# Attention in head pairs on the halves of TensorE, with a fused score-and-maximum operation and an early opening of the output projection

## What is computed

```
scores = (q @ k.T) * HEAD_DIM ** -0.5 + bias        # per head; 256 queries, causal
p = exp(scores - max(scores)); p = p / sum(p)
o = p @ v
x = x + concat(o) @ w_o
```

## Time and profile before

| what | value |
|---|---|
| median of 3 runs | 1553.88 us (1550.59 to 1556.39) |
| the profiled execution: time | 1550.96 us |
| the profiled execution: span of the core | 1549.2 us |
| TensorE busy | 1468.2 us, 95% of the span |
| VectorE busy | 780.3 us, 50% |
| ScalarE busy | 573.7 us, 37% |
| mean granted TensorE clock | 0.983 |

### The profile page before, as it was taken

One profiled execution on the slowest core, in us unless ns is written; L12 is line 12 of the kernel. 1 busy time (PEld: TensorE's weight loads), 2 busy tenths in 40 slices (PEclk: granted clock), 3 DMA queues, 4 the chain that ended last, 5 costly groups with the idle time before them and its releaser, 6 DMA issues.

```text
span 1549.2 us, 28384 instructions
## 1 busy us (share of the span) xinstructions
PE 1468.2 (95%) x11254; PEld 1225.1 (79%) x11254; DVE 780.3 (50%) x1409; ACT 573.7 (37%) x929; POOL 294.6 (19%) x121
## 2 busy tenths in 40 slices
PE   7978999999999999999999999999999999989996
PEld 5857999999958999998999898998666666555553
DVE  4954888637674898733453645653322222212122
ACT  2244555445344655436655116444211111111110
POOL 0021222212201121233865001673000000000000
PEclk9989999999999999998999999999999999999998
DMA  8674455574534455652544212477999999999995
GB/s 312 234 275 157 163 164 173 191 255 139 164 137 136 147 174 184 203 175 82 177 137 137 69 55 74 166 256 268 427 424 426 423 425 426 426 427 424 423 426 222
DMA packets 72097, 375.82 MB, mean 243 GB/s; under 512 B 8128, under 2 KB 8384, under 8 KB 49984
## 3 DMA queue, kind: packets, MB, share of 16 engines
q1 hardware_dynamic: 72000, 374.43, 64.1%
HBM read 373.35 MB, written 1.05 MB: 242 GB/s over the span
## 4 chain that ended last, share of the span: by engine, by line
PE 61%; issue 13%; DVE 8%; DMA 8%; SPq 7%; ACT 2%; POOL 1%; POOLq 0%; DVEq 0%; ACTq 0%
PE lin L692 9%; PE lin L693 8%; PE lin L694 8%; DMA moe_low<-in_experts 7%; PE stat L1394 4%; PE mixp L1367 4%; PE mixp L1371 4%; SPq L609 4%; DVE mixers L2034 3%; PE lin L711 2%; PE stat L1327 1%; PE lin L1337 1%; PE stat L692 1%; PE mixp L692 1%; PE stat L693 1%
## 5 line engine op out<-in xcount | busy, mean ns | idle before, releaser
L692 PE MATMUL lin<-r_hi,w_hi 128*128 128x256 f32 x1464 | 426.4, 291 | 11.8 <-POOL w_lo L1838 5.1
L693 PE MATMUL lin<-r_lo,w_hi 128*128 128x256 f32 x1464 | 416.6, 285 | 0.0
L694 PE MATMUL lin<-r_hi,w_lo 128*128 128x256 f32 x1464 | 416.5, 284 | 0.0
L692 PEld LDWEIGHTS lin<-r_hi,w_hi 128*128 128x128 f32 x1464 | 283.4, 194 | 19.8 <-POOL w_lo L1838 6.7
L693 PEld LDWEIGHTS lin<-r_lo,w_hi 128*128 128x128 f32 x1464 | 283.4, 194 | 0.8
L694 PEld LDWEIGHTS lin<-r_hi,w_lo 128*128 128x128 f32 x1464 | 283.2, 193 | 0.0
L1842 POOL TENSOR_TENSOR w_lo<-ring,w_hi 128x1024 fp32r<-128x1024 f32 x71 | 175.4, 2482 | 199.3 <-ACT w_hi L1435 199.2
L1838 POOL TENSOR_TENSOR w_lo<-ring,w_hi 128x1024 fp32r<-128x1024 f32 x42 | 108.3, 2578 | 480.2 <-ACT w_hi L1441 297.9
L1871 DVE TENSOR_TENSOR w_lo<-ring,w_hi 128x1024 fp32r<-128x1024 f32 x126 | 156.5, 1247 | 84.9 <-ACT w_hi L1441 65.1
L1441 ACT ACTIVATE w_hi<-ring 128x1024 fp32r<-128x1024 f32 x124 | 129.6, 1049 | 57.3 <-PE mixp L694 49.0
L1435 ACT ACTIVATE w_hi<-ring 128x1024 fp32r<-128x1024 f32 x119 | 124.1, 1050 | 34.1 <-PE lin L694 16.7
(11 more groups left out here) (485 smaller groups left out, 2795.1 us busy)
## 6 DMA issues: line engine op xcount, KB each, us to landing
ring<-in_panels SPq DMA_DIRECT2D x272, 512.0 KB, 3.8
moe_low<-in_experts SPq DMA_DIRECT2D x64, 1024.0 KB, 22.6
moe_high<-in_experts SPq DMA_DIRECT2D x22, 2048.0 KB, 24.9
aring<-in_ada SPq DMA_DIRECT2D x24, 1024.0 KB, 6.3
ring<-in_experts SPq DMA_DIRECT2D x20, 1024.0 KB, 26.6
moe_high<-in_experts SPq DMA_DIRECT2D x20, 1024.0 KB, 21.9
cst<-in_experts SPq DMA_DIRECT2D x10, 1280.0 KB, 23.5
sq<-in_experts SPq DMA_DIRECT2D x10, 1024.0 KB, 29.5
```

The lines of the kernel that those rows point to most:

```text
L692: pe.matmul(o, w_hi[:, slot, c], r[0], start=start, stop=False, skip_group_check=True)
L693: pe.matmul(o, w_hi[:, slot, c], r[1], start=False, stop=False, skip_group_check=True)
L694: return pe.matmul(o, w_lo[:, slot, c], r[0], start=False, stop=stop, skip_group_check=True)
```

## The change

The attention loop goes over eight pairs of heads. Scores of both heads of a pair are issued alternately, on the two row halves and in two banks; the outputs of both heads alternately on the two column halves of one bank. In PE's order the scores of the next pair come first, then the outputs of the pair two back, the modulation group, and the transposes of the pair before. On VectorE one fused operation per block, `tensor_tensor_reduce`, adds the bias (now eight times as large), scales by minus one eighth, writes the negated scores and their minimum; ScalarE's exponential takes them with scale -1. The two heads' probabilities are scaled by one operation per block, with a broadcast reciprocal. Two `w_lo` splits of the output projection's panels are placed in turns 1 and 2. The first two panels of the projection are done tile by tile: six tiles before the last pair is transposed, one before its outputs, one after. The even layer's projection now opens with two panels as well.

```diff
-        "bias00": pattern_bias(0, 0), "bias10": pattern_bias(P, 0), "bias11": pattern_bias(P, P),
+        "bias00": HD ** 0.5 * pattern_bias(0, 0), "bias10": HD ** 0.5 * pattern_bias(P, 0), "bias11": HD ** 0.5 * pattern_bias(P, P),
...
+            def open_project(tiles, rows, first, last):
+
+                if first:
+                    for j in range(2):
+                        bank(split_panel(j))
+                for i in tiles:
+                    for j in range(2):
+                        b = (panels.n + j) % RING
+                        mm = split_matmul(lin[b][:, 0:T], (b, slice(i * P, (i + 1) * P)), [t[:, i, :] for t in rows],
+                                          first and i == tiles[0], last and i == tiles[-1])
+                        if last and i == tiles[-1]:
+                            mm.then_inc(panel_done, 1)
+                if last:
+                    panels.advance(2)
...
             pe.wait_ge(r_split, 1 + KH)
+            open_project(range(KD), (r_hi, r_lo), True, True)
             project((r_hi, r_lo))
...
+            def score_pair(j):
+
+                if j:
+                    pe.wait_ge(scores_read, j)
+                for part in range(2):
+                    for n in range(2):
+                        q, k = (qk1[64 * n:64 * n + 64, t, :] for t in (j, 8 + j))
+                        if part == 0:
+                            pe.matmul(mixbank(n)[:, 0:P], q[:, 0:P], k[:, 0:P], start=True, stop=True, skip_group_check=True)
+                        else:
+                            mm = pe.matmul(mixbank(n)[:, P:3 * P], q[:, P:T], k, start=True, stop=True, skip_group_check=True)
+                mm.then_inc(scores_ready, 1)
+
+            def outputs(g):
+
+                pe.wait_ge(pt_copied, 2 * g + 2)
+                if g >= 2:
+                    pe.wait_ge(o_copied, g - 1)
+                for c in range(3):
+                    for n in range(2):
+                        head = 2 * g + n
+                        o = lin[g % 2][64 * n:64 * n + 64, (0 if c == 0 else P):(P if c == 0 else T)]
+                        mm = pe.matmul(o, vt1[:, c // 2, head * HD:(head + 1) * HD],
+                                       pt1[:, 2 * (g % 2) + n, c * P:(c + 1) * P], start=c < 2, stop=c != 1, skip_group_check=True)
+                mm.then_inc(o_ready, 1)
+
+            def turn_probs(g):
+
+                pe.wait_ge(probs_ready, g + 1)
+                for n in range(2):
+                    if g:
+                        pe.wait_ge(pt_copied, 2 * g - 1 + n)
...
+            score_pair(0)
+            for j in range(PAIRS):
+                if j + 1 < PAIRS:
+                    score_pair(j + 1)
+                if j >= 2:
+                    outputs(j - 2)
+                modulation(lin[2], 16 + j, 1)
+                if j >= 1:
+                    turn_probs(j - 1)
+            outputs(PAIRS - 2)
+            pe.wait_ge(o_copied, PAIRS - 2)
             pe.wait_ge(modrow_ready, 3)
+            open_project(range(0, PAIRS - 2), (r_hi, r_lo), True, False)
+            turn_probs(PAIRS - 1)
+            pe.wait_ge(o_copied, PAIRS - 1)
+            open_project([PAIRS - 2], (r_hi, r_lo), False, False)
+            outputs(PAIRS - 1)
+            pe.wait_ge(o_copied, PAIRS)
+            open_project([PAIRS - 1], (r_hi, r_lo), False, True)
             project((r_hi, r_lo))
...
-                    if i == HEADS:
-                        split_hi(OUT1 + 1)
-            split_hi(OUT1 + 4)
-            modulation_row(lin[2][:, :], 2)
+            for j in range(HEADS // 2 + 1):
+                if j < HEADS // 2:
+                    act.wait_ge(scores_read, j + 1)
+                    if j >= 2:
+                        act.wait_ge(pt_ready, 2 * j - 2)
...
+                if j:
+                    g = j - 1
+                    for n in range(2):
+                        act.wait_ge(pt_ready, 2 * g + n + 1)
+                        if g >= 2:
+                            act.wait_ge(o_ready, g - 1)
+                        act.activation(pt1[:, 2 * (g % 2) + n, :], statbank(n)[:, 0:SC], ACT.Copy).then_inc(pt_copied, 1)
+                if j == HEADS // 2 - 1:
+                    modulation_row(lin[2][:, :], 2)
...
+            for j in range(HEADS // 2 + 2):
+                if j < HEADS // 2:
...
+                    for n in range(2):
+                        for c, (a0, a1) in enumerate(((0, P), (P, 3 * P))):
+                            m = 2 * (2 * j + n) + c
+                            ins = dve.tensor_tensor_reduce(s1[:, 2 * (j % 2) + n, a0:a1], mixbank(n)[:, a0:a1], bias[:, a0:a1],
+                                                           -HD ** -0.5, 3e38, ALU.add, ALU.min, mx1[:, m:m + 1])
+                    ins.then_inc(scores_read, 1)
+                if j in (1, 2):
+                    split_lo(OUT1 + 1 + j)
+                if 1 <= j <= HEADS // 2:
...
+                    link(dve.reciprocal(r1[:, 4 * g:4 * g + 4], l1[:, 4 * g:4 * g + 4]))
                     for c, (a0, a1) in enumerate(((0, P), (P, 3 * P))):
+                        ins = dve.tensor_tensor(p1[:, pair, a0:a1], p1[:, pair, a0:a1],
+                                                per_row(r1, g, c).unsqueeze(2).broadcast_to([P, 2, a1 - a0]), ALU.mult)
                     ins.then_inc(probs_ready, 1)
+                if j >= 2:
+                    g = j - 2
+                    dve.wait_ge(o_ready, g + 1)
+                    split_rows(g, lin[g % 2][:, 0:T]).then_inc(o_copied, 1)
             split_lo(OUT1 + 4)
```

More of the change, by code:

```diff
@@ L777, in route @@
                     mm.then_inc(ev("logits_ready"), 1)
+            def open_project(tiles, rows, first, last):
[11 more added lines that the diff above has]
+                    panels.advance(2)
             def project(rows, first=False):
                 if first:
-                    opening = [split_panel(j) for j in range(2)]
-                    for b in opening:
-                        bank(b)
                     for i in range(KD):
                         pe.wait_ge(h_ready, seen(h_ready))
-                        for b in opening:
-                            mm = split_matmul(lin[b][:, 0:T], (b, slice(i * P, (i + 1) * P)), [t[:, i, :] for t in rows],
-                                              i == 0, i == KD - 1)
-                            if i == KD - 1:
-                                mm.then_inc(panel_done, 1)
-                    panels.advance(2)
-                for m in range(2 if first else 0, KD):
+                        open_project([i], rows, i == 0, i == KD - 1)
+                for m in range(2, KD):
                     b = split_panel()
@@ L989, in _ @@
             pe.wait_ge(qk_ready, 16)
-            for i in range(HEADS + 3):
-                if i < HEADS:
-                    if i >= 2:
-                        pe.wait_ge(scores_read, i - 1)
-                    o = 64 * (i % 2)
-                    q, k = qk1[o:o + 64, i // 2, :], qk1[o:o + 64, 8 + i // 2, :]
-                    pe.matmul(mixbank(i)[:, 0:P], q[:, 0:P], k[:, 0:P], start=True, stop=True, skip_group_check=True)
-                    pe.matmul(mixbank(i)[:, P:3 * P], q[:, P:T], k, start=True, stop=True, skip_group_check=True)\
-                        .then_inc(scores_ready, 1)
-                if i < HEADS and i % 2 == 1:
-                    modulation(lin[2], 16 + i // 2, 1)
-                if 2 <= i <= HEADS + 1:
-                    g = i - 2
-                    pe.wait_ge(probs_ready, g + 1)
-                    if g >= 2:
-                        pe.wait_ge(pt_copied, g - 1)
+            def score_pair(j):
[9 more added lines that the diff above has]
+                mm.then_inc(scores_ready, 1)
@@ L1008, in _ @@
                     mm.then_inc(pt_ready, 1)
-                if i >= 3:
-                    g = i - 3
-                    pe.wait_ge(pt_copied, g + 1)
-                    if g >= 4 and g % 2 == 0:
-                        pe.wait_ge(o_copied, g // 2 - 1)
-                    o = lin[(g // 2) % 2][64 * (g % 2):64 * (g % 2) + 64, :]
-                    v = [vt1[:, c, g * HD:(g + 1) * HD] for c in range(NT)]
-                    pe.matmul(o[:, 0:P], v[0], pt1[:, g % 4, 0:P], start=True, stop=True, skip_group_check=True)
-                    pe.matmul(o[:, P:T], v[0], pt1[:, g % 4, P:2 * P], start=True, stop=False, skip_group_check=True)
-                    pe.matmul(o[:, P:T], v[1], pt1[:, g % 4, 2 * P:3 * P], start=False, stop=True, skip_group_check=True)\
-                        .then_inc(o_ready, 1)
@@ new lines, in per_row @@
+            def per_row(ap, j, c):
+                return ap[:, 4 * j:4 * j + 4].rearrange("p (n c) -> p n c", c=2)[:, :, c]
+            for j in range(HEADS // 2 + 2):
+                if j < HEADS // 2:
+                    pair = slice(2 * (j % 2), 2 * (j % 2) + 2)
+                    dve.wait_ge(scores_ready, j + 1)
+                    if j >= 2:
```

(18 more changed lines are left out.)

45 lines of the change are left out of this document (5 added, 40 removed).

## The result

The changed kernel takes 1536.81 us (median of four runs, 1533.74 to 1539.82), the kernel before in the same comparison 1552.24 (1549.60 to 1556.39): ratio 0.9911, 95% interval 0.9891 to 0.9932, 15.4 us less. The prediction had 1546.6 with a range down to 1542.5. It had the sign and the mechanism of the loop; it missed the size by more than its range allowed. A second comparison of the same two kernels (experiment 8) gives 13.3 us and a ratio of 0.9912.

What follows compares the result with a forecast made beforehand. It took PE's instruction stream to bound the attention loop; changed, a loop through DVE sets 4.11 us a pair. First two panels done at 42.35 instead of 49.7, -7.3 us, took the median from 1553.88 to 1546.6; range 1542.5 to 1553.

Steps and rivals of the forecast that it cites:

- TensorE's sums: TensorE's work per pair: scores 0.85, outputs 0.78, modulation 1.00, transposes 0.84 us, in all 3.47 instead of 5.24.
- rival 4: Row and column halves don't overlap: scores 1.70, outputs 1.60, period 5.8 us, time 1558.4; chance 0.03.
- The loop that closes: Scores, outputs, rounding and fused operations wait on each other in turn: 4.11 us a pair, PE idle about 0.6.
- F: VectorE's fused score operations for one pair of heads, with their accumulator read-outs: taken as 1.45 us.
- The bounds 1.13 to 1.9: Limits for F in us: the cost of the maxima alone, or that plus a full accumulator read-out for each operation.
- rival 3: Read-outs on VectorE are free, F = 1.13: period 3.8 us, -9.6, time 1544.3; chance 0.15.
- the prediction's own slope of 7: Each us on F costs about 7 us of kernel time, one for each pair but one.
- Rival 2: Fused VectorE operations dearer: 1549.8 us at F 1.9, 1554.5 at half rate; chance 0.13 for 1.7 to 2.4, 0.05 beyond.
- Fill and drain: Loop's start and end: two weight splits of 1.22 us on the path, scores 7 at 25.9, last rounding ending at 41.6.
- The edits at no cost: Even layer's two-panel opening, removed ACT splits and earlier panel loads: no effect on the time.
- rival 5: Granted clock falls because PE idles in the loop: +1.5 to 1.7 us a time, 1548.2; chance 0.10.
- the sum: From first score product to the first two projection panels done: 42.35 us instead of 49.7, so -7.3 us.

Runs made afterwards that it cites:

- experiment 8: The changed kernel run again unaltered, 1537.80 us, ratio 0.9912 to the kernel before; both kernels were also profiled again, to three profiles each.
- experiment 2: The changed kernel with the rounding of a pair's outputs one turn later in VectorE's queue: 1536.00 us, ratio 0.9909 to the kernel before.
- experiment 5: The changed kernel with the rounding one turn later and the two weight splits out of turns 1 and 2: 1536.46 us, ratio 0.9921.
- experiment 3: The changed kernel with the even layer's first two panels opened one after the other: 1537.74 us, ratio 0.9917 to the kernel before.

## Why the prediction was wrong

- **TensorE's sums** (0.85, 0.78, 1.00, 0.84) were right within 0.04: measured 0.85, 0.81, 1.00, 0.88. Halves overlap; rival 4 is out.
- **The loop that closes** was right: PE waits before the scores on the fused line, for 0.28 to 0.44 instead of 0.6, and experiment 2 shows by cutting it that this loop sets the period. The period is 3.82 to 3.98 instead of 4.11.
- **F was mis-sized,** the term "read-outs at 0.08, F = 1.45": it measures 1.20. The read-outs take 83 ns each but run beside the next operation. The bounds 1.13 to 1.9 held it, and rival 3 (F = 1.13) was the nearer of the two. By the prediction's own slope of 7, that is 1.75 us. Rival 2, the half rate, is out; the Trainium skill's rule (Vector Engine (DVE) Microarchitecture Reference, section 7) that the fused form with two non-bf16 SBUF sources runs at half rate is not touched, since one source is PSUM here; applied all the same it would have misled, for 256 columns took 0.42.
- **Fill and drain** were right in sum: with F at 1.20 the forecast 41.6 for the last tile becomes 39.85, measured 39.8 (40.0 and 39.7 in the other two profiles). The loop's gain is then 7.3 + 1.75 = 9.05, measured 9.0 (70.7 against 61.7). A part of this agreement is luck: the last scores start 23.7 to 24.0 behind the first where the forecast gives 24.15, and from there to the last tile it is 16.0 instead of 15.7. The splits in turns 1 and 2 stand on the path, but moving them gave 0.7 for both in experiment 5, where the rounding was moved as well; the forecast had put 2.44 on the path.
- **The edits at no cost** cost nothing (experiment 3). That earlier loads of the next panels bring nothing was not tried by itself.
- **The clock (rival 5)** fell once in the loop of two of the three profiles of the changed kernel, and cost almost nothing there: the loop took 32.05 and 32.31 us at 0.95 and 31.95 at 1.00. With TensorE waiting for VectorE, slower products fill the idle time. In two profiles of the kernel before with delays it fell too, and there, bound by TensorE, the loop took 45.4 and 50.0 us instead of 43.8. The price of 1.5 to 1.7 a time fits the first of these, and was wrong for a loop that another engine bounds.
- **The step that failed** is the one that the sum does not state. It ends at the second panel, adds that "the six later panels are the same products at the same rate", and puts every stage behind them at nothing. The quoted sentence held: from there to the norm the two kernels differ by some 0.2 us. The unspoken one did not: of the 15.4 us, 6.4 came from stages that the change does not touch (4.3 by the second comparison, 5.6 by the three pairs of profiles). F alone, 1.75 us, would not have left the range. Shown: the norm's stage is 170.7 us in all profiles of the kernel before and 164.9 to 169.2 in the changed one, at a higher granted clock for equal products; the other two rows of the table, 1.7 and 0.9, scatter by as much as they differ, and the stop at the end is 0.3 to 0.8 us shorter. Shown too: the kernel before gains as much from 1.7 us of empty work, though 3.3 us of that is the stop at the end, which the changed kernel keeps. Estimated: the fit through the 14 runs of the kernel before in the first set gives 0.9 us for each 0.001 of mean clock; the changed kernel's ten runs have 0.985 and the kernel before 0.983, so some 2 us are mean clock. Why the norm's stage is slower in the kernel before, undelayed, is open.

The sum: forecast 1546.6; minus 1.6 for the kernel before's own median (1552.24 beside the 1553.88 the forecast started from), minus 1.8 for F, minus 6.4 for the stages behind, gives 1536.8. It closes by construction, since the 6.4 is what is left of 15.4 once the loop's 9.0 is taken off.

## What to carry to other kernels

A gain inside one stage moves all later stages in time, and where the granted clock moves by itself that can be worth half as much as the edit. Added or removed instructions also move everything behind them in an engine's instruction list, which was worth 3.3 us here. Before crediting or blaming an edit for less than about half a per cent, run both kernels with one or two small delays and see how far the time strays from the line, and compare the profiles stage by stage, up to the last instruction, before naming a cause for it. Read the edit's own worth between two landmarks that enclose it, here 9.0 us to within 0.3 in every profile. And when a loop closes through one engine's queue, look at what stands ahead of the urgent operation there: moving one rounding back made the loop 2.0 us shorter, almost as much as fusing three operations of a head into two.

## What the runs showed of the hardware

- The fused two-source operation with a minimum reads f32 PSUM and f32 SBUF as fast as a maximum alone reads its one source: 285 ns for 128 columns and 419 for 256, where the maxima took 286 and 410. The next operation starts 0.20 and 0.35 us later, and the read-out of 83 ns runs beside it.
- Six products of 128 columns (twelve instructions) in column halves take 0.81 us, four score products (eight instructions) on two row halves 0.85.
- A VectorE product of two SBUF sources (128x512) that starts 10 to 20 ns behind a GpSimd product takes 0.69 or 2.88 us; which of the two is not settled by the start times in the records (20 ns behind in two of the slow cases and 10 in the third, and both among the quick ones).
- 1.7 us of products that nothing reads made a 1550 us kernel 6.4 us faster, 4.3 us of them cost nothing. In both profiles, 3.3 us less go with a stop of 2.3 us in TensorE's last 16 instructions, beside packets of the instruction queues, that is gone when products are added ahead. The stop keeps its place in the instruction order in every execution of a kernel, and two added products moved it by four instructions.
- From the experts' first product until 2 MB are left to move, the DMA engines carry 425 GB/s at a share of 1.01, and the stretch takes 434.4 to 435.1 us in six profiles of the two kernels, whatever happened ahead of it.
